# Expert stage: one loop over eight experts, eight slots in which the remainder overwrites the raw weights, four rounded ones

## What is computed

```
logits = u @ w_router                       # u: 256 tokens x 1024
top_logit, top_e = top_k(logits, 2); top_w = softmax(top_logit)
# tokens are gathered by expert into blocks of 128 slots
y_block = (silu(xe @ w1[e]) * (xe @ w3[e])) @ w2[e]     # w1, w3: 1024 x 2816, w2: 2816 x 1024
y = zeros.at[slot_tok].add(y_block * slot_w)
```

## Time and profile before

| | us |
|---|---|
| median of 3 runs | 3135.72 |
| lowest, highest | 3135.0, 3139.96 |
| the profiled execution, its own time | 3138.09 |
| span of the profiled execution | 3136.4 |
| expert stage, from about 2247 to 3118 | some 870 |
| PE busy in the span | 2739.4 (87%) |

### The profile page before, as it was taken

How to read it: one execution, slowest core, us unless ns; L and a number is a source line. 1 busy time by engine, 2 the same in 40 slices (tenths; PEclk the granted TensorE clock), 3 DMA queues, 4 the chain that set the end, 5 groups by cost and what they waited for, 6 DMA issues and landing times. The chain is left out here.

```text
span 3136.4 us, 35052 instructions
## 1 busy us (share of the span) xinstructions
PE 2739.4 (87%) x12871; PEld 2178.0 (69%) x12871; DVE 1451.2 (46%) x1832; ACT 1285.7 (41%) x1532; POOL 1511.7 (48%) x600
## 2 busy tenths in 40 slices
PE   4987999899888699996868898979599999999997
PEld 2774778687557588875665676747587777777775
DVE  2386312431422323202364324331477787778776
ACT  2421332331332333312421523333366676667765
POOL 0330344143123344433321643606198888879986
PEclk6988999999999899998888999989699999999999
DMA  6236233132112133321235532504399999989996
GB/s 193 81 121 202 81 89 93 34 89 86 41 41 81 42 95 99 99 81 55 71 104 163 146 94 81 146 15 121 122 339 316 320 338 331 324 312 335 347 311 241
DMA packets 271658, 492.34 MB, mean 157 GB/s; under 512 B 14576, under 2 KB 102928, under 8 KB 271376
## 3 DMA queue, kind: packets, MB, share of 16 engines
q1 hardware_dynamic: 271288, 490.18, 47.8%
q10 hardware_dynamic: 216, 0.07, 0.0%
HBM read 489.16 MB, written 1.05 MB: 156 GB/s over the span
## 5 line engine op out<-in xcount | busy, mean ns | idle before, releaser
L279 POOL TENSOR_TENSOR unit_lo<-raw_units,unit_hi 128x1024 fp32r<-128x1024 f32 x248 | 592.5, 2410 | 1123.3 <-ACT unit_hi L271 1123.3
L2114 POOL TENSOR_TENSOR moe_unit_lo<-moe_raw,moe_unit_hi 128x640 fp32r<-128x640 f32 x266 | 739.8, 2808 | 162.4 <-ACT moe_unit_hi L2109 162.2
L2114 DVE TENSOR_TENSOR moe_unit_lo<-moe_raw,moe_unit_hi 128x1408 fp32r<-128x1408 f32 x266 | 541.5, 2044 | 180.4 <-ACT moe_unit_hi L2109 179.0
L2109 ACT ACTIVATE moe_unit_hi<-moe_raw 128x2048 fp32r<-128x2048 f32 x266 | 510.1, 1919 | 275.7 <-PE bank L300 268.8
L271 ACT ACTIVATE unit_hi<-raw_units 128x1024 fp32r<-128x1024 f32 (+1 forms) x250 | 247.6, 1039 | 750.4 <-PE bank L300 584.5
L298 PE MATMUL bank<-unit_hi,hT_hi 128*128 128x512 f32 x880 | 352.0, 400 | 41.0 <-POOL unit_lo L279 13.6
L299 PE MATMUL bank<-unit_lo,hT_hi 128*128 128x512 f32 x880 | 348.1, 396 | 0.0
L300 PE MATMUL bank<-unit_hi,hT_lo 128*128 128x512 f32 x880 | 347.9, 395 | 0.0
L298 PE MATMUL bank<-moe_unit_hi,xe_T_hi 128*128 128x512 f32 (+1 forms) x768 | 297.0, 387 | 12.0 <-DVE moe_unit_lo L2114 8.5
L300 PE MATMUL bank<-moe_unit_hi,xe_T_lo 128*128 128x512 f32 (+1 forms) x768 | 289.5, 377 | 0.0
L299 PE MATMUL bank<-moe_unit_lo,xe_T_hi 128*128 128x512 f32 (+1 forms) x768 | 288.9, 376 | 0.0
(11 more groups left out here) (370 smaller groups left out, 4445.5 us busy)
## 6 DMA issues: line engine op xcount, KB each, us to landing
moe_raw<-in_moe_w SPq DMA_DIRECT2D x270, 1024.0 KB, 5.2
raw_units<-in_w_in SPq DMA_DIRECT2D x160, 512.0 KB, 3.8
ada_unit<-in_ada_w SPq DMA_DIRECT2D x40, 1024.0 KB, 5.3
raw_units<-in_ffn_w SPq DMA_DIRECT2D x66, 512.0 KB, 3.7
raw_units<-in_w_branch SPq DMA_DIRECT2D x48, 512.0 KB, 3.7
ada_first<-in_ada_w SPq DMA_DIRECT2D x8, 1024.0 KB, 12.0
raw_units<-in_w_out SPq DMA_DIRECT2D x16, 512.0 KB, 3.7
constants<-in_consts SPq DMA_DIRECT2D x1, 1124.0 KB, 5.2
```

What stands on the lines that cost most here:

```text
L279: eng.tensor_tensor(lo, whole, hi.bitcast(F32), ALU.subtract).then_inc(lo_ready, 1)
L2109: act.activation(moe_hi[:, v % RING, :], moe_raw[:, raw_slot(x, v), :], ACT.Copy).then_inc(hi_m, 1)
L2114: eng.tensor_tensor(moe_lo[:, s, a:b], moe_raw[:, raw_slot(x, v), a:b], moe_hi[:, s, a:b].bitcast(F32), ALU.subtract).then_inc(done, 1)
```

## The change

It concerns the expert stage alone.

- There are eight raw slots (`SLOTS`) and `moe_lo` lies on the same addresses: the remainder overwrites the raw unit. `moe_hi` has four slots, `AHEAD` is 3. Six loads are issued in the routing stage as before (`EARLY`), two more at the start of the expert stage.
- A load waits until PE has used the unit that was in the slot (`used`), not until it was split.
- DVE subtracts all 2048 columns. POOL subtracts nothing; it copies the expert's column of the route and builds `pick` for the next expert (`build_pick`), behind `put_sum` of this one.
- The body of each engine's loop holds all eight experts, the loop turns `passes` times, and the addresses of the loads are constants.
- ACT writes `ye[0]` rounded from the banks in two halves, DVE subtracts `ye[1]` from the banks in two halves; `ytmp` isn't written.
- After the last expert eight units of expert 0 are loaded that nobody uses; before it were six.

```
-        RAW_RING, RING, AHEAD = 6, 3, 2
-        moe_lo = at("moe_unit_lo", [P, RING, 2048], F32R, R0 + (RAW_RING + RING) * 8192)
+        SLOTS, RING, AHEAD, EARLY = 8, 4, 3, 6
+        moe_raw = at("moe_raw", [P, SLOTS, 2048], F32, R0)
+        moe_lo = at("moe_unit_lo", [P, SLOTS, 2048], F32R, R0)
+        moe_hi = at("moe_unit_hi", [P, RING, 2048], F32R, R0 + SLOTS * 8192)
...
-            def lo(eng, i, x, v, a, b, done):
-                eng.tensor_tensor(moe_lo[:, s, a:b], moe_raw[:, raw_slot(x, v), a:b], moe_hi[:, s, a:b].bitcast(F32), ALU.subtract).then_inc(done, 1)
+            def lo(dve, i, x, v):
+                at_unit = U * x + v
+                dve.wait_ge(hi_m, NE * U * i + at_unit + 1)
+                dve.tensor_tensor(moe_lo[:, at_unit % SLOTS, :], moe_raw[:, at_unit % SLOTS, :],
+                                  moe_hi[:, at_unit % RING, :].bitcast(F32), ALU.subtract).then_inc(lo_m, 1)
...
+            def build_pick(pool, nn):
+                pool.tensor_copy(column[:, :, :], route[:, 0:2, :, bass.ds(nn, 1)].rearrange("p a j e -> p a (j e)")).then_inc(column_out, 1)
+                pool.wait_ge(column_out, nn + 1)
+                pool.sem_inc(pick_turn, 1)
                 for j in range(2):
+                    pool.tensor_scalar(pick[:, j, :], const("iota"), column[:, 0, j:j + 1], column[:, 1, j:j + 1],
+                                       ALU.is_equal, ALU.mult).then_inc(pick_ready, 1)
+                pool.wait_ge(pick_ready, 3 * nn + 2)
+                pool.sem_inc(pick_turn, 1)
+                pool.tensor_copy(pick_r[:, :, :], pick[:, :, :]).then_inc(pick_ready, 1)
...
-                    with sp.Fori(0, passes * (NE // 2)) as i:
-                                sp.wait_ge(lo_dve, split)
-                                sp.wait_ge(lo_pool, split)
+                    for v in range(EARLY, SLOTS):
+                        load_moe(sp, 0, v)
+                    with sp.Fori(0, passes) as i:
+                        for x in range(NE):
+                            for v in range(SLOTS, U + SLOTS):
+                                sp.wait_ge(used, sp.snap(NE * U * i + (U * x + v - SLOTS + 2)))
                                 sp.sem_inc(slot_free, 1)
+                                load_moe(sp, x, v)
...
-                            act.activation(ytmp[:, 0:512], ps[6][:, :], ACT.Copy, scale=w_slot[:, 0:1])
-                            act.activation(ytmp[:, 512:D], ps[7][:, :], ACT.Copy, scale=w_slot[:, 0:1]).then_inc(ye_out, 1)
+                            act.wait_ge(combined, 4 * n + 4)
+                            for half in range(2):
+                                act.activation(ye[0][:, half * 512:(half + 1) * 512], ps[6 + half][:, :], ACT.Copy,
+                                               scale=w_slot[:, 0:1]).then_inc(ye_out, 1)
...
-                                lo(dve, i, x, u + AHEAD, 0, CUT, lo_dve)
+                                lo(dve, i, x, u + AHEAD)
...
-                            dve.wait_ge(ye_out, n + 2)
-                            step(dve, dve.tensor_copy(ye[0][:, :], ytmp[:, :]))
-                            dve.tensor_tensor(ye[1][:, :], ytmp[:, :], ye[0][:, :].bitcast(F32), ALU.subtract).then_inc(ye_ready, 1)
+                            dve.wait_ge(ws_out, n + 1)
+                            for half in range(2):
+                                cs = slice(half * 512, (half + 1) * 512)
+                                dve.wait_ge(ye_out, 2 * n + half + 3)
+                                dve.scalar_tensor_tensor(ye[1][:, cs], ps[6 + half][:, :], w_slot[:, 0:1], ye[0][:, cs].bitcast(F32),
+                                                         ALU.mult, ALU.subtract).then_inc(ye_ready, 1)
```

More of the change, by code:

```diff
@@ L1926, in program @@
         U = len(plan)
-        assert U % RING == 0 and 2 * U % RAW_RING == 0
-        raw_m = [sem(f"moe_raw_loaded{i}") for i in range(RAW_RING)]
+        assert NE * U % RING == 0 and NE * U % SLOTS == 0
+        raw_m = [sem(f"moe_raw_loaded{i}") for i in range(SLOTS)]
         def unit_part(buf, slot, v):
@@ L1962, in _ @@
                     sp.dma_start(wr[:, :, :], t["moe_router"][0].rearrange("(k p) n -> p k n", p=P)).then_inc(router_in, 16)
-                    for v in range(RAW_RING):
-                        load_moe(sp, 0, 0, v)
+                    for v in range(EARLY):
+                        load_moe(sp, 0, v)
                     sp.wait_ge(router_in, 16)
@@ L2096, in moe_experts @@
+            (hi_m, lo_m, used, column_out, pick_ready, gathered, xe_act, xe_dve, put_sum,
              put_out, ws_out, silu_out, g_done, turned, hi_out, lo_done, ye_out, ye_ready,
[L2097 to L2105, removed]
-            def hi(act, i, x, v):
-                act.wait_ge(raw_m[raw_slot(x, v)], 16 * (2 * U // RAW_RING) * i + 16 * ((U * x + v) // RAW_RING + 1))
-                act.activation(moe_hi[:, v % RING, :], moe_raw[:, raw_slot(x, v), :], ACT.Copy).then_inc(hi_m, 1)
@@ L2130, in build_pick @@
-            def build_pick(dve, step, nn):
-                for j in range(2):
[L2133 to L2136, removed]
+             combined, added, slot_free, pick_turn) = (stage_sem(s) for s in names)
@@ L2190, in _ @@
                     passes = pool.value_load(n_pass[0:1, 0:1], min_val=1, max_val=2)
-                    for v in range(AHEAD):
-                        lo(pool, 0, 0, v, CUT, 2048, lo_pool)
-                    with pool.Fori(0, passes * (NE // 2)) as i:
-                        for x in range(2):
-                            for v in range(AHEAD, U + AHEAD):
-                                lo(pool, i, x, v, CUT, 2048, lo_pool)
+                    build_pick(pool, 0)
+                    with pool.Fori(0, passes) as i:
+                        for x in range(NE):
+                            n = NE * i + x
+                            pool.wait_ge(put_sum, n + 1)
+                            pool.sem_inc(pick_turn, 1)
+                            build_pick(pool, n + 1)
                 @block.scalar
@@ L2210, in _ @@
                         xe_out(copy, 0, p, 0, xe_act, act)
-                    with act.Fori(0, passes * (NE // 2)) as i:
-                        for x in range(2):
-                            n = 2 * i + x
+                    with act.Fori(0, passes) as i:
+                        for x in range(NE):
+                            n = NE * i + x
                             for u in range(U):
@@ L2296, in _ @@
                         gather(pe, 0, p)
-                    with pe.Fori(0, passes * (NE // 2)) as i:
-                        for x in range(2):
-                            n = 2 * i + x
+                    with pe.Fori(0, passes) as i:
+                        for x in range(NE):
+                            n = NE * i + x
                             pe.wait_ge(xe_act, 2 * n + 2)
```

70 lines of the change are left out of this document (25 added, 45 removed).

## The result

The changed kernel takes 3102.27 us (median of four runs, 3100.0 to 3107.35) against 3137.84 us of the kernel before, measured beside it: a ratio of 0.9889 with a 95% interval of 0.9872 to 0.9907, or 35.6 us less. The forecast was 3108 us, 27.7 us less, with a range of 3088 to 3125. The sign and the range held; the gain was 8 us larger than the sum says.

What follows compares the result with a forecast made beforehand. PE was taken as the bound, busy 102.2 of 106 us per expert. Gains of 33.4 us less costs of 5.7 gave 27.7 us net, from 3138.1 to 3110.4, or 3108 us as the runs' median; range 3088 to 3125.

Steps and rivals of the forecast that it cites:

- (1): PE's waits for splits go, as AHEAD rises from 2 to 3 units: 11.2 us gained.
- (3): One loop over eight experts instead of four turns of two: three turns' "issue" waits go, 2.3 us gained.
- (4): PE's wait for moe_gT_lo goes, since POOL instead of DVE builds pick: 2.4 us gained.
- (2): POOL's split pace in the projections no longer holds PE: 0.25 us per group of four units, 11.0 us gained.
- (5): The clock's fall to 0.93 behind the 1.72 us split wait at three expert boundaries goes: 5.0 us gained.
- (7): Waits for additions into moe_y grow: before the third combine 9.4 to 12.0 us, second pair 1.6 to 3.6; cost 2.6 + 2.0.
- (8): Start of the expert stage: DVE has three splits instead of two ahead of xe_T_hi; cost 1.1 us, between 0 and 3.6.
- (6): Tail: the last combine's 4.53 us wait falls to about 3.0 with ye written and subtracted in halves: 1.5 us gained.
- (9): Loads wait until PE has used the slot's unit; with eight slots the cost is zero if DMA keeps the pace.
- B: Rival: the clock falls behind the longer wait before the third combine; 11 us more, 3119 us. Chance 14%.
- C: Rival: DMA becomes the bound at 328 to 331 GB/s, 104.5 us per expert; 3123 us. Chance 11%.
- E: Rival: DVE's split costs 2.91 us, making DVE the bound at 109.5 us per expert; 3164 us. Chance 7%.

Runs made afterwards that it cites:

- b_dve_alone: The kernel before with DVE subtracting all 2048 columns and POOL nothing; loop of two experts, AHEAD 2, six slots kept: 3108.66 us, ratio 0.9904.
- a_ahead2: The changed kernel with AHEAD 2 instead of 3: 3098.77 us, ratio 0.9873 to the kernel before.
- a_pool_share: The changed kernel with POOL again subtracting columns 1408 to 2047 and building pick between its splits: 3132.15 us, ratio 0.9981 to the kernel before.
- a_pool_share_dve_pick_ahead2: The changed kernel with POOL again subtracting columns 1408 to 2047, pick built by DVE, and AHEAD 2: 3125.73 us, ratio 0.9966 to the kernel before.
- b_unroll: The kernel before with only the loop body changed, from two experts to all eight; POOL still shares the split: 3142.9 us, ratio 1.0023.
- a_add_first: The changed kernel with DVE's additions into moe_y ahead of the split in steps u = 2 and 3: 3086.23 us, ratio 0.9839 to the kernel before.

## Why the prediction was right, step by step

**Right in sign and in the waits.** The waits that (1), (3) and (4) take away, 11.2 + 2.3 + 2.4 us, have no row in after. But (1) gave the third unit of lead as the reason, and that is one of three that each suffice between the experts. b_dve_alone has neither lead nor slots and no wait for a split, and a_ahead2 keeps its period: there it is the shorter split. a_pool_share shares the split, has three units of lead and no such wait there. a_pool_share_dve_pick_ahead2 has neither, only less work on ye, and waits for a split just behind pick. (3) has no gain of its own while POOL shares (b_unroll), and 6.5 us by the stage time, 2 by the medians, once it doesn't.

**Where the sum was off.** The prediction said that the waits list gives all the places where PE stands still. It doesn't: by the stage times 34.5 us, less 15.9 (waits), 5.0 (clock) and 1.5 (tail), plus 0.6 and 1.3 (costs), leave 14.0 us of gain that no row shows. The starts of PE's matmuls tell where they lie. The first matmul of unit 4, the fifth transposes, the last matmul of the expert and the next unit 4, first before, then after (the timeline of PE):

```profile
2386.17 0.49 PE L298 MATMUL bank<-moe_unit_hi,xe_T_hi 128*128 128x512 f32 x1
...
2438.27 0.60 PE L2348 MATMUL bank<-constants,moe_prod 128*128 128x128 f32 x4
...
2473.68 0.39 PE L300 MATMUL bank<-moe_unit_hi,moe_gT_lo 128*128 128x512 f32 x1
...
2491.26 0.48 PE L298 MATMUL bank<-moe_unit_hi,xe_T_hi 128*128 128x512 f32 x1
```

```profile
2385.89 0.48 PE L298 MATMUL bank<-moe_unit_hi,xe_T_hi 128*128 128x512 f32 x1
...
2437.16 0.60 PE L2334 MATMUL bank<-constants,moe_prod 128*128 128x128 f32 x4
...
2471.31 0.39 PE L300 MATMUL bank<-moe_unit_hi,moe_gT_lo 128*128 128x512 f32 x1
...
2487.07 0.48 PE L298 MATMUL bank<-moe_unit_hi,xe_T_hi 128*128 128x512 f32 x1
```

In this expert the projections take 52.10 us before and 51.27 after, the down projection with its gathers 35.41 and 34.15, and the way to the next unit 4 17.58 and 15.76 (19.3 and 15.7 where the kernel before does not turn its loop). Over the whole stage, with the forecast's terms sorted into the same stretches:

| stretch | terms | forecast gain, us | measured, us |
|---|---|---|---|
| projections, units 4 to 21 | 4.5 of the 5.5 groups of (2) | 9.0 | 6.1 |
| down projection | eight short waits in (1), 2.7; (4), 2.4 | 5.1 | 9.8 |
| between experts | the rest of (1) and (2); (3), (5), less (7) | 13.2 | 20.3 |
| start | (8) | -1.1 | -1.3 |
| behind the last unit | (6) | 1.5 | -0.5 |

**(2)** The groups start 11.35 us apart, as said. Before, they were 11.58 apart in the mean, so 0.23 of the 0.25 us a group came back where a whole group was measured; but the units at both ends of the projections lost less. The term was a third too large there.

**(4), priced by its wait row.** DVE builds pick in the down projection, and behind it PE stood twice, 0.35 us for a split and 0.3 for moe_gT_lo; in the starts of the matmuls that stretch costs 1.2 us an expert, twice what the two rows show. Either cure alone is enough: with pick still on DVE but POOL off the split (b_dve_alone) the down projections take 273.2 us in all, as in after, and with pick on POOL but POOL sharing (a_pool_share, three units of lead) 273.6, against 283.0 before.

**Restarts.** Between the experts the gain is 7 us larger than the terms. By the waits of PE 4 of them are (7), which was over-sized, see below. The rest stands in no row: each wait costs PE more than its row, as the removed 1.45 us of a_add_first did.

**(5)** The clock is 1.00 at the boundaries, as said, and a fall costs about what it was priced at: some 3.4 us at 1.2 GHz (0.72 from 2587 to 2593 us), with matmuls 0.43 us apart instead of 0.23. But it gains nothing by itself. Where the clock fell before, the wait before the third combine was short, 0.41 us instead of 1.98:

```profile
2592.88 0.50 PE L2162 MATMUL bank<-moe_ye_hi,put 128*128 128x512 f32 x1 [0.41 <-DVE moe_y L2169]
```

From the last matmul of one expert to unit 4 of the next, PE takes 19.33, 19.39 and 19.31 us with a fall, and 19.30 at the fourth such boundary (2367 to 2391 us), which has the same 1.72 us wait and a clock of 1.00. So (5) is in truth the other side of the 9.4 us in (7), which the falls had made small; the two belong together. And the wait for a split is often, not always, followed by a fall. In b_unroll the clock is 0.93 at four of the six boundaries from 2470 to 3029 us and 1.00 at the other two, though each has that wait. Of the four falls two cost 1.0 us of the same stretch and two 0.1. Two of the boundaries (columns as in the earlier trace rows):

```profile
2791.00:2815.00 24.00, 20.24 (x81) 14.96 (x80) 20.57 (x12) 12.17 (x10) 13.94 (x7) 0.93 0.84 287
2898.00:2922.00 24.00, 19.99 (x85) 14.61 (x84) 20.66 (x13) 13.66 (x10) 15.08 (x7) 1.00 0.85 292
```

**(6)** The last wait went from 4.53 to 3.0 us: 1.5, as said. But from the last matmul of the last unit to the end of the span it is 27.85 us after and 27.40 before. There the granted clock of after is 0.53 from 3080 to 3090 us, and that of before was still 1.00 from 3108 to 3114 us; what made it fall earlier, no run tells.

**(7)** Half right. The wait before the third combine is 11.4 us against 12.0 said (+2.0 instead of +2.6). The one before the transposed pick was to grow from 1.6 to 3.6 us; in PE's list it fell to 0.2, and in the starts of the matmuls it is the 0.29 x 8 = 2.3 us above. By the waits of PE this half was over-sized by 3.4 us: the second additions lie mostly beside unit 3.

**(8)** From the end of the routing to the first matmul of the split units the stage is 1.25 us longer, against 1.1. a_ahead2 confirms what does it.

**(9)** No row of ACT waiting for a load in after: right.

**The rivals.** B did not happen: the wait of 1.25 to 1.46 us is there in all experts and the clock stays at 1.00. C did not: 343 GB/s in after, 351 in a_add_first. The figure of 330 to 340 GB/s that the Trainium skill gives for transfers of 1 MiB (SBUF — State Buffer, The DMA setup-cost knee) is passed where loads stand in line. E did not: 2.29 us a split, in place or not. F did not in after; but b_unroll, which was slower, shows that the long body is no free gain. D did not happen as it was told, since the wait before the third combine stayed; a_add_first, which removes it, gives 16 us more instead of D's 12.

## What to carry to other kernels

An engine that helps with a part of each unit has its own time for it, and here it lengthened the other's: look first whether the work fits on one engine (here 33 x 2.29 us in an expert of 100 us), and take the helper off before adding buffers and lead. Count what such a change is worth from the starts of the bound engine's instructions, stretch by stretch; its wait rows left out 14 us of 34.5. Then read what stands ahead of the short operation that the bound engine waits for; exchanging two statements gave 16 us (against after) on top of the 35.6 of the whole change. Lead is not free: one more unit ahead is one more unit of work in front of everything else in that engine's list.

## What the runs showed of the hardware

- **DVE and POOL on one subtraction.** The least that DVE takes for 1408 columns is 1.61 us, and POOL for 640 columns 1.54, at the start of the stage where the other doesn't split; beside each other DVE's median is 2.0 to 2.2 us, up to 3.0, and POOL's 2.95. DVE alone for all 2048 columns takes 2.29 us, so with the helper a split was ready each 2.93 us and without it could be each 2.29. In b_unroll:

```profile
L2114 POOL TENSOR_TENSOR moe_unit_lo<-moe_raw,moe_unit_hi x266: 1537/2956/3023, 2250.4 to 3116.0; 128x640 fp32r<-128x640 f32 x133
L2114 DVE TENSOR_TENSOR moe_unit_lo<-moe_raw,moe_unit_hi x266: 1610/2008/3000, 2254.9 to 3115.5; 128x1408 fp32r<-128x1408 f32 x133
```

  The Trainium skill (SBUF — State Buffer, Who interferes with whom) calls the port pair of the two engines an exclusive lock. Strictly in turn a unit would take 1.61 + 1.54 = 3.15 us (an estimate from the rows above); POOL's pace of 2.93 us is 7% under it, so the trace agrees with a lock nearly, but not to the full length of both instructions. I had cited this rule only against rival E, and had priced what sharing costs PE at 11.0 us. Taking POOL off the split gave 28.2 us by the stage time, of which the projections, where that pace was counted, have 6.1.
- **A loop's turn on ACT** costs two table loads of 1.28 us, one at the body's head and one at the first silu; each adds about 1.30 us between two operations of ACT (in b_dve_alone the second starts at 2473.95, the silu at 2475.24).
- **DMA** sustained 351 GB/s over 740 us of 1 MB loads, with PE busy throughout.
